# Prompt attention on Trainium2: the order of VectorE's two halves of a unit, and the place of five stores

## The reference, cut to what matters

```
u = rms_norm(x) ; z = u @ W_in                       # projection: q, k, v, gates
A = fox_attention(q, k, v, cumulative log forget)    # 8 heads
B = g0*compressed + g1*selected + g2*window          # 8 query heads, 2 key/value groups
h = x + (sigmoid(ga)*(A@U_A) + sigmoid(gb)*(B@U_B)) @ W_out
y = h + expert_layer(rms_norm(h))                    # top-1 of 4 groups, top-2 of 8 experts
# returned too: the projected keys and values of all tokens, and log forget
```

## Time and profile before

| | before |
|---|---|
| the profiled execution | 2397.16 us |
| its span | 2395.0 us |
| PE busy | 2049.4 us (86%) |
| DVE, ACT, POOL busy | 528.7, 239.7, 107.8 us |
| mean granted clock of PE | 0.927 of 2.4 GHz |
| compress, to | about 227 us |
| project, to | about 671 us |
| prompt, to | about 933 us |
| decode, to | about 1461 us |

### The profile page before, as it was taken

The page is one execution under the profiler, slowest core; times in us unless marked ns, Lnnn a source line. Parts: engine busy times, 40 slices in busy tenths (PEclk is TensorE's granted clock), DMA queues, the critical chain, the costliest instruction groups (busy, mean ns, idle before and its releaser), DMA issues. The chain is left out here.

```text
span 2395.0 us, 33992 instructions
## 1 busy us (share of the span) xinstructions
PE 2049.4 (86%) x13747; PEld 1245.9 (52%) x13747; DVE 528.7 (22%) x1099; ACT 239.7 (10%) x621; POOL 107.8 (4%) x124
## 2 busy tenths in 40 slices
PE   7999999999988778989999998999954677877763
PEld 7887677777765554545555556763432232323321
DVE  2544122224232332111111110110041111111112
ACT  0001111111102221000000000000010000000000
POOL 0000000000000000000000000000001121121111
PEclk9999999999989999999999999999976788888876
DMA  7654643332231124999999996423276999999998
GB/s 264 196 176 146 242 173 128 135 106 88 106 135 63 62 87 159 407 373 372 383 399 389 368 391 260 167 106 135 76 313 278 395 411 414 412 411 391 405 414 334
DMA packets 167985, 614.98 MB, mean 257 GB/s; under 512 B 31780, under 2 KB 89653, under 8 KB 132469
## 3 DMA queue, kind: packets, MB, share of 16 engines
q1 hardware_dynamic: 125742, 545.19, 58.7%
q0 software_dynamic: 22800, 45.07, 5.2%
q10 hardware_dynamic: 19288, 22.55, 2.9%
HBM read 702.95 MB, written 39.60 MB: 310 GB/s over the span
## 5 line engine op out<-in xcount | busy, mean ns | idle before, releaser
L520 PE MATMUL bank<-ut,wring 128*128 128x320 f32 x1408 | 385.6, 434 | 1.1 <-PEq L208 1.1
L520 PEld LDWEIGHTS bank<-ut,wring 128*128 128x128 f32 x1408 | 267.8, 191 | 112.0 <-issue 3.4
L1218 PE MATMUL bank<-ut,zt 128*128 128x320 f32 x576 | 179.1, 449 | 19.0 <-DMA zt<-in_w_gate 11.6
L2106 PE MATMUL bank<-wdn,par 128*32 128x512 f32 x512 | 90.7, 843 | 115.7 <-issue 112.4
L827 PE MATMUL bank<-ut,wring 128*128 128x320 f32 x448 | 149.8, 461 | 0.6 <-DVE ncum L1071 0.6
L1218 PEld LDWEIGHTS bank<-ut,zt 128*128 128x128 f32 x576 | 102.6, 190 | 91.3 <-issue 46.1
L2077 PE MATMUL bank<-wgu,arena 128*32 128x512 f32 x1024 | 119.0, 605 | 0.8 <-DVE arena L2157 0.8
L1545 PE MATMUL bank<-wring,arena 128*128 128x512 f32 x256 | 112.0, 595 | 3.1 <-DVE arena L1585 1.6
L683 DVE RECIPROCAL selmask<-selmask 128x320 f32<-128x320 f32 x30 | 64.5, 2149 | 201.4 <-ACT selmask L657 201.4
L827 PEld LDWEIGHTS bank<-ut,wring 128*128 128x128 f32 x448 | 83.3, 200 | 28.7 <-issue 9.1
L2106 PEld LDWEIGHTS bank<-wdn,par 128*32 128x32 f32 x512 | 18.5, 134 | 148.7 <-issue 144.7
(11 more groups left out here) (414 smaller groups left out, 2299.5 us busy)
## 6 DMA issues: line engine op xcount, KB each, us to landing
wgu<-in_w_gu SPq DMA_DIRECT2D x128, 1024.0 KB, 14.7
wdn<-in_w_dn SPq DMA_DIRECT2D x32, 2048.0 KB
arena<-in_kv_v SPq DMA_DIRECT2D x88, 640.0 KB, 8.9
arena<-in_kv_k SPq DMA_DIRECT2D x84, 640.0 KB, 8.9
wring<-in_w_proj SPq DMA_DIRECT2D x44, 1024.0 KB, 4.9
wring<-in_w_merge SPq DMA_DIRECT2D x32, 1024.0 KB, 4.9
wring<-in_kv_k SPq DMA_DIRECT2D x44, 640.0 KB, 9.2
wring<-in_kv_v SPq DMA_DIRECT2D x40, 640.0 KB, 9.6
```

Source lines behind the costliest of these rows:

```text
L520: last = nc.tensor.matmul(m.bank[:, 2 + s % 2, 0:T], m.wring[:, s, k * P:(k + 1) * P], m.ut[:, k, :], start=(k == 0), stop=(k == KD - 1))
L1218: last = nc.tensor.matmul(m.bank[:, 7, 0:T], m.gw[n % 2][:, k // 2, k % 2 * P:(k % 2 + 1) * P], m.ut[:, k, :], start=(k == 0), stop=(k == ...
L2106: last = nc.tensor.matmul(m.bank[j * TW:(j + 1) * TW, 6 + i % 2, :], e.hid[:, i % 2, f * TW:(f + 1) * TW], w[:, f, cols:cols + 512], start ...
```

## The change

Two edits. In the project stage SP no longer issues the five stores, nor waits for `v_ready`, `zn_ready` and `rope_ready` before them; it issues them in the prompt stage, behind the four rows of constants. In the prompt stage DVE's loop does `back(u-1)` ahead of `front(u)`.

```diff
             for s in range(3):
                 sp.wait_ge(z_done, NW - SLOTS + s + 1)
                 sp.dma_start(m.wring[:, s, :], a["w_gate"][s, :, :]).then_inc(m.gw_in[s], 16)
-            sp.wait_ge(v_ready, NV)
-            for t in range(2):
-                sp.dma_start(a["v_prompt"][t * P:(t + 1) * P, :], m.vt[:, t, :, :].rearrange("p j d -> p (j d)")
-                             ).then_inc(m.stores, 16)
-            sp.dma_start(a["v_sample"], m.vt[0:TS, 2, :, :].rearrange("p j d -> p (j d)")).then_inc(m.stores, 16)
-            sp.wait_ge(zn_ready, NQK)
-            sp.dma_start(a["k_fox"], m.zt[:, FK:FK + FH, :]).then_inc(m.stores, 16)
-            sp.wait_ge(rope_ready, NQK - NQ)
-            sp.dma_start(a["k_nsa"], m.zt[:, CK:NQK, :]).then_inc(m.stores, 16)
...
                 sp.dma_start(dst, a["consts"][0:dst.shape[0], at:at + n]).then_inc(m.rows_in, 16)
+            for t in range(2):
+                sp.dma_start(a["v_prompt"][t * P:(t + 1) * P, :], m.vt[:, t, :, :].rearrange("p j d -> p (j d)")
+                             ).then_inc(m.stores, 16)
+            sp.dma_start(a["v_sample"], m.vt[0:TS, 2, :, :].rearrange("p j d -> p (j d)")).then_inc(m.stores, 16)
+            sp.dma_start(a["k_fox"], m.zt[:, FK:FK + FH, :]).then_inc(m.stores, 16)
+            sp.dma_start(a["k_nsa"], m.zt[:, CK:NQK, :]).then_inc(m.stores, 16)
...
             for u in range(NU + 1):
+                if u >= 1:
+                    back(u - 1)
                 if u < NU:
                     front(u)
-                if u >= 1:
-                    back(u - 1)
```

## The result

The changed kernel takes 2339.83 us (median of 4 runs, 2335.60 to 2343.02) against 2397.93 us (4 runs, 2389.71 to 2403.21): ratio 0.9752, 95% interval 0.9733 to 0.9771. That is 58.1 us less, where 60 were forecast (2337, range 2325 to 2356). The profiled execution has a span of 2337.8 us, 57.2 less than before.

A forecast was written before the change was run, and what follows sets the result against it. The prediction took the prompt unit loop as bound by hand-overs, PE waiting for DVE's `back`. Gains of 4.5 (edge) + 40.2 (waits) + 5.0 (overlap) + 10.3 (clock) = 60.0 us took 2397.2 to 2337.2 us, range 2325 to 2356.

The forecast's parts named there:

- The bound: Prompt unit loop: bound by a chain of hand-overs; 40.2 of PE's 41.3 us idle are waits for line 1113.
- The three terms of the loop: Prompt unit loop: PE's waits 40.2, lost matmul overlap 5.0 and slower clock 10.3 us, together 55.5 us gained.
- The waits: Prompt unit loop: PE's 31 waits for line 1113, the end of `back`, vanish whole, gaining 40.2 us.
- The clock: Prompt unit loop: without waits the granted clock rises from 0.95 to 1.00, gaining 10.3 us, bounds 0 and 11.3.
- The tails: Prompt unit loop: each of 31 waits also costs 0.16 us of matmul overlap, 5.0 us in all, bounds 0 and 5.
- The margin: Prompt unit loop: DVE and ACT's longest chain takes 3.9 us against PE's 5.0, a margin of 1.1 us.
- The edge: Between project and prompt stages: without the stores the stage ends with DVE, gaining 4.5 us, bounds 3.4 and 5.6.
- the step that decode shifts whole: Decode: paced by its loads, which begin with it, so prompt savings move it forward whole without shortening it.
- The clock that stays: Rival, unit loop: the waits go but clock falls have another cause, so the clock stays; 2347.5 us, chance 0.20.
- Half of the waits back at another place: Rival, unit loop: PE waits at transposes or copied probabilities, half of the 55.5 us lost; 2365 us, chance 0.10.
- The order that does nothing: Rival, unit loop: PE waits for something else at the same moment, only the edge gains; 2392.7 us, chance 0.04.
- The slower case: Rival, unit loop: the new cycle closes in series through ACT, period 6.5 us over 6.2; 2413 us, chance 0.04.

The follow-up runs named there:

- x7_delay10: Changed kernel with ten more DVE instructions in each `back`, on data that nothing reads; 2410.24 us, ratio 1.0049 against the kernel before.
- x6_delay6: Changed kernel with six more DVE instructions in each `back`, on data that nothing reads; 2358.34 us, ratio 0.9819 against the kernel before.
- x5_delay2: Changed kernel with two more DVE instructions in each `back`, on data that nothing reads; 2337.9 us, ratio 0.9738 against the kernel before.
- x2_stores_only: Changed kernel with DVE's old loop order, so only the five stores are moved; 2391.71 us, ratio 0.997 against the kernel before.
- x1_order_only: Kernel before with only DVE's loop order turned round, stores left in the project stage; 2340.43 us against 2399.4, ratio 0.9762.

## Why the prediction was right

**The bound.** Right. The waits for line 1113 were what PE lacked; with them the loop lost 56.03 us, 55.5 forecast. PE's idle time in it went from 41.3 us to 1.1, and those 1.1 are the edge to decode in both.

**The three terms of the loop.** The waits: 40.2 us forecast, and all are gone. The clock: 10.3 forecast; the loop's clock is 1.00 in the eight kernels with 0 to 16.6 us of waits and 0.89 to 0.95 in the four with 39 to 45. `x7_delay10` shows that waits alone, without the old order, bring the falls back. The prediction's evidence against this term, 536 to 540 us in project at 0.50 with PE busy all the time, was read too narrowly: the clock was at 0.50 from 532 us on, and in the 8 us up to 536 PE was busy for 6.14 only. Busy time by stretch, of the kernel before:

```profile
528.00:532.00 4.00, 2.92 (x25) 2.68 (x24) 0.90 (x2) 0.71 (x2) 0.00 (x0) 1.00 0.61 219
532.00:536.00 4.00, 3.22 (x17) 3.03 (x15) 0.69 (x1) 0.00 (x0) 0.00 (x0) 0.50 0.12 47
```

So this fall, too, came with pauses of PE.

The tails: 0.16 us a wait forecast. 56.03 - 40.2 - 10.3 = 5.5 us over 31 waits is 0.18; `x7_delay10` gives about 0.15, `x6_delay6` 0.33 a listed wait or 0.21 a late hand-over. The clock has two digits here, so that term and the tails are known together, and each alone only to about 1 us.

**The margin.** I worked out 1.1 us from the longest mix of kinds, and the trace has 0.4 to 3.4, 1.9 on the mean. That was a bound on the safe side: the chain of DVE and ACT costs 3.4 us for `slc` and `win`, not 3.9, because the unit with the long `back` (`cmp`) has the short `front`. `x5_delay2` used 0.66 us of it for nothing, `x6_delay6` with 1.98 us went over it in 18 units.

**The edge.** 4.5 us forecast, 4.65 measured, and `x2_stores_only` has it alone. The issues behind it were hidden, with 7.2 us in hand and not 2.3: I had taken the 6.18 us for the four rows over from before, and they were long only because the stores stood ahead of them. The third load of gate weights was issued at 709.34, 709.3 forecast.

**The rest.** The forecast took nothing for it. The stretch before the units lost 0.58 us, which is within what it varies by, 52.8 to 55.3 us in the ten kernels with the moved stores. There is a fall of the clock behind the edge as before, 0.57 from 668 to 672 us now and 0.57 and 0.58 from 668 to 676 then, though PE pauses for 0.97 us instead of 5.62. Decode took 3.6 us more in this trace. It did not do so in `x1_order_only` (524.2) or with the stores alone (525.8), so the step that decode shifts whole was right, and 3.6 us is within what decode varies by from trace to trace. Loop and edge together gave 60.7 us, and the other stretches took 3.5 back. As decode alone varies by 7.5 us among the kernels with 14 tiles, a total within 2 us of the forecast is in part luck.

**The rivals.** The clock that stays (2347.5) is out, as the loop's clock is 1.00; that the waits were the cause of the falls is shown by `x7_delay10`. Half of the waits back at another place is out by the list of waits, which has none of PE's within the loop. The order that does nothing (2393) is out by `x1_order_only`, which has 59.0 us less. The slower case would have needed the copies of ACT in series with the new cycle; PE finds each of them ready.

## What to carry to other kernels

In an in-order queue, do first what ends a chain, then what starts the next one: the input of `back` was ready while DVE sat idle for scores, and swapping two lines was worth 2.4%. Price such a wait by three terms: its idle time, the overlap lost at its ends, and the slower clock in the stretch around it, which came with 39 us of waits and more here and not with 16.6. And when a loop goes from bound by waits to bound by work, look again at what had been put into it as filling: here two gate tiles fewer were worth nothing in the old order and 17 us in the new one.

## What the runs showed of the hardware

The granted clock does not fall in proportion to idling, and short pauses are enough for it to fall. With 16.6 us of waits in a loop of 173 us it stayed at 1.00; with 40.2 us in 207, none longer than 2.3, it was 0.95; with 42.3 us in 221 it was 0.89; with 45.1 in 199 it was 0.92.

A DMA's issue can be slow because of what was issued ahead of it: four small loads took SP 6.18 us behind five stores of about 4.5 MB, in the kernel before and in `x1_order_only`, and 1.38 us ahead of them, in the changed kernel and in `x2_stores_only`.
